# The state recurrence of a hybrid decoder layer's RWKV-7 mixer: chunk updates formed as affine maps for all chunks, then one scan over the three head pairs together

## The reference, cut to what matters

```
def step(S, inp):
    r_t, w_t, k_t, v_t, kk_t, a_t = inp
    sa = jnp.einsum('bhvk,bhk->bhv', S, -kk_t)
    S = (S * w_t[:, :, None, :]
         + sa[..., None] * (kk_t * a_t)[:, :, None, :]
         + v_t[..., None] * k_t[:, :, None, :])
    return S, jnp.einsum('bhvk,bhk->bhv', S, r_t)
```

## Time and profile before

| | |
|---|---|
| time, median of 3 runs | 876.85 us (874.28 to 879.99) |
| the profiled execution | 877.97 us, of which the span is 876.2 us |
| mean granted TensorE clock | 0.994 |
| PE busy | 840.4 us of the span |
| DVE, ACT, POOL busy | 281.8, 191.1, 101.3 us |
| meta recurrence and the three pairs | about 146.6 to 333.7 us of the span |

### The profile page before, as it was taken

The page is one execution under the profiler, slowest core; times in us unless marked ns, Lnnn a source line. Parts: engine busy times, 40 slices in busy tenths (PEclk is TensorE's granted clock), DMA queues, the critical chain, the costliest instruction groups (busy, mean ns, idle before and its releaser), DMA issues.

```text
span 876.2 us, 16200 instructions
## 1 busy us (share of the span) xinstructions
PE 840.4 (96%) x6939; PEld 473.6 (54%) x6939; DVE 281.8 (32%) x578; ACT 191.1 (22%) x380; POOL 101.3 (12%) x216
## 2 busy tenths in 40 slices
PE   9999999989999899899999999999999979999995
PEld 8888888766766454454544444444445533333331
DVE  5245710322323324712222434444411233121212
ACT  4224101131235122403121112080022201111110
POOL 8840000000005000111000000000000010222211
PEclk9999999999999999999999999999999999999998
DMA  7322146000000000481111111065390296999972
GB/s 218 89 60 85 49 96 195 2 3 3 3 2 2 3 27 25 99 204 48 49 48 49 49 48 49 25 240 166 122 358 26 76 399 245 326 389 394 388 254 99
DMA packets 76135, 109.76 MB, mean 125 GB/s; under 512 B 16891, under 2 KB 61067, under 8 KB 71968
## 3 DMA queue, kind: packets, MB, share of 16 engines
q1 hardware_dynamic: 71296, 93.22, 31.5%
q0 software_dynamic: 4768, 15.52, 6.1%
HBM read 100.32 MB, written 10.50 MB: 126 GB/s over the span
## 4 chain that ended last, share of the span: by engine, by line
PE 89%; DVE 4%; issue 2%; DMA 2%; ACT 1%; SPq 0%; POOL 0%; DVEq 0%; POOLq 0%; ACTq 0%
PE ps L1554 18%; PE ps L1922 10%; PE ps L1449 8%; PE ps L1531 8%; PE ps L1868 6%; PE ps L1621 6%; PE ps L1829 5%; PE ps L1948 5%; PE ps L1536 5%; PE ps L1748 1%; PE ps L1814 1%; PE ps L1909 1%; PE ps L1433 1%; PE ps L1788 1%; PE ps L1766 1%
## 5 line engine op out<-in xcount | busy, mean ns | idle before, releaser
L1554 PE MATMUL ps<-arena 128*128 128x512 f32 x304 | 141.3, 602 | 0.4 <-DMA arena<-in_w_in 0.4
L1554 PEld LDWEIGHTS ps<-arena 128*128 128x128 f32 x304 | 54.2, 189 | 62.1 <-issue 59.0
L1922 PE MATMUL ps<-arena 128*32 128x512 f32 x624 | 86.2, 599 | 0.5 <-DVE arena L1338 0.5
L1449 PE MATMUL ps<-arena 128*128 128x264 f32 x320 | 72.7, 386 | 0.0
L1449 PEld LDWEIGHTS ps<-arena 128*128 128x128 f32 x320 | 60.0, 189 | 11.6 <-ACT arena L757 0.7
L1531 PE MATMUL ps<-arena,h 128*128 128x264 f32 x256 | 63.4, 393 | 0.0
L1621 PE MATMUL ps<-arena 64*64 64x64 f32 x2208 | 50.9, 221 | 9.1 <-issue 5.2
L1621 PEld LDWEIGHTS ps<-arena 64*64 64x64 f32 x2208 | 44.6, 134 | 26.3 <-issue 18.5
L1868 PE MATMUL ps<-arena 128*128 128x512 f32 x128 | 56.2, 594 | 0.0
L1829 PE MATMUL ps<-yT_all,arena 128*128 128x512 f32 x112 | 50.2, 600 | 1.1 <-DMA arena<-in_w_p_fox 1.1
L1531 PEld LDWEIGHTS ps<-arena,h 128*128 128x128 f32 x256 | 46.6, 188 | 8.6
(11 more groups left out here) (349 smaller groups left out, 1023.5 us busy)
## 6 DMA issues: line engine op xcount, KB each, us to landing
arena<-in_moe_w_down SPq DMA_DIRECT2D x32, 512.0 KB, 6.0
arena<-in_moe_w_gate SPq DMA_DIRECT2D x13, 1024.0 KB
arena<-in_moe_w_up SPq DMA_DIRECT2D x13, 1024.0 KB
arena<-in_w_in SPq DMA_DIRECT2D x19, 512.0 KB, 3.8
arena<-in_w_in SPq DMA_DIRECT2D x5, 1024.0 KB, 6.5
h<-in_x SPq DMA_DIRECT2D x8, 512.0 KB, 5.8
arena<-in_w_out SPq DMA_DIRECT2D x1, 4096.0 KB, 13.2
h<-in_w_in SPq DMA_DIRECT2D x3, 1024.0 KB, 5.3
```

What stands on the lines that cost most here:

```text
L1449: ins = mm(ps[:, 2 * (n % 2) + hf, 0:HALF], w[:, c, j * P:(j + 1) * P], nT[:, c, hf * HALF:(hf + 1) * HALF], start=(c == 0), stop=(c == DC ...
L1554: ins = mm(ps[:, gate_bank(n), :], weights_of_gate(n)[:, c, :], nT[:, c, META:L], start=(c == 0), stop=(c == DC - 1))
L1922: ins = mm(ps[rs, bank, :].rearrange("p (h n) -> p h n", h=2), xgT[:, s, c, rs], w1[ws][:, :, c, :], start=(c == 0), stop=(c == DC - 1))
```

## The change

For each pair, instead of the scan, three further products are formed for all chunks at once, so that chunk c acts on its incoming state S as an affine map: new S = M S + K and y = R S + Y0.

- `w2`'s batch gets a second product (KtT x VT, the first half of K). After it come one batch of two products (M from W1 and BtT; first half of Y0), one of two products (R from W1 and RBT; second half of Y0) and one of a single product (second half of K): 16 + 32 + 32 + 16 matmuls more for each pair. DVE turns three of the results into place (`Rt`, `Bt`, `Kt`; 512 columns each), ACT copies Y0 out. Three steps of filler (`AFFINE_FILL`) stand behind them. The next pair's second turn batch waits for the DVE and ACT results.
- The scan then runs once, over the 8 chunks, with the three pairs inside: for each pair 2 matmuls for the state (not at the last chunk) and 2 for y, and one DVE operation for the new state. One step of `fill` follows each chunk. y is gathered in one PSUM bank for each pair and added to Y0 by DVE at the end (512 columns, three times).
- The six norms move from the scan of p = 1 into levels 3, 4, 5 of p = 1 and 1, 2, 3 of p = 2, in the place of 2 steps of `fill_qkv` each. With that and the scans' filler gone, `HEAD_FILL` grows from 111 to 139 steps. The gate filler behind the first two head sums shrinks from 5 and 8 steps to 3 and 7; those three steps are the filler behind the last pair's products.
- The two heads of a pair come out on swapped partition halves. So the bonus is copied with halves swapped (two copies for one), `ln_g` and `ln_b` load in four DMAs instead of two, and the RWKV projection weights in two DMAs for each block, so that a block takes 6 DMAs.

```
-        scan_fill = lambda p, c: (2, 0 if 1 <= c <= 6 else 4 if c == NCH - 1 else 2, 0)[p]
+        level_fill = lambda p, lv: (0 if (p, lv) in NORM_AT else 2) + LEVEL_FILL
...
+                for i in range(2):
+                    sp.dma_start(wpr[dc % 2][64 * i:64 * i + 64, 0:3, :], wp_r[:, cs].rearrange("(c h p) n -> h p c n", h=2, p=HD)[1 - i]).then_inc(s, 16)
...
                     groups_out(("H", p, lv))
+                    if (p, lv) == (1, 2):
+                        key_or_query_squares(0)
+                    if (p, lv) in NORM_AT:
+                        m = NORM_AT.index((p, lv))
+                        norm_root(m)
+                        if m < 5:
+                            key_or_query_squares(m + 1)
...
+                act.wait_ge(sem("q_psum"), p + 1)
+                done(a.activation(flat(Y0s[p]), ps[:, 6, :], ACT.Copy), "y0_ready")
+            act.wait_ge(sem("y_out_rwkv"), RC)
...
-            done(v.tensor_copy(tc_[:], tb[:]), "bonus_moved")
+            done(v.tensor_copy(tc_[0:64], tb[64:128]))
+            done(v.tensor_copy(tc_[64:128], tb[0:64]), "bonus_moved")
...
+                dve.wait_ge(sem("q_psum"), p + 1)
+                done(tt(body(Rt, p), body(Rt, p), bank(5), ALU.add), "affine_ready")
+                dve.wait_ge(sem("d_psum"), p + 1)
+                done(tt(body(Bt, p), bank(4), bc(ident2[:]), ALU.add), "affine_ready")
+                done(tt(body(Kt, p), bank(1), ends(p).broadcast_to([P, NCH, CH]), ALU.mult), "affine_ready")
+            for c in range(NCH - 1):
+                for p in range(RC):
+                    dve.wait_ge(sem("s_psum"), 1 + RC * c + p + 1)
+                    done(stt(Ss[p][:, c, :], ps[:, (0, 1, 4)[p], 0:CH], ends(p)[:, c, :], body(Kt, p)[:, c, :], ALU.mult, ALU.add), "S_ready")
...
+            for p in range(RC):
+                dve.wait_ge(sem("y_psum"), p + 1)
+                done(tt(yT[0][:, p, :], ps[:, 5 + p, :], Y0s[p].rearrange("p n t -> p (n t)"), ALU.add), "y_out_rwkv")
...
+                if p >= 1:
+                    pe.wait_ge(sem("affine_ready"), 3 * p)
+                    pe.wait_ge(sem("y0_ready"), p)
+                side_by_side((4, cm(Bt), cm(At), 0, 0), (6, cm(At), idq, 0, 1)).then_inc(sem("nt_psum"), 1)
...
-                side_by_side((0, um(TTm), um(Hm), 1, 0)).then_inc(sem("w2_psum"), 1)
+                side_by_side((0, um(TTm), um(Hm), 1, 0), (1, um(KtT), um(VT), 0, 0, "first")).then_inc(sem("w2_psum"), 1)
...
+                side_by_side((4, um(W1), um(BtT), 0, 0), (6, um(VT), um(RKT), 0, 1, "first"))
+                side_by_side((5, um(W1), um(RBT), 0, 0), (6, um(W2), um(RBT), 0, 1, "then")).then_inc(sem("q_psum"), 1)
+                side_by_side((1, um(BtT), um(W2), 0, 0, "then")).then_inc(sem("d_psum"), 1)
+                more(AFFINE_FILL)
+            pe.wait_ge(sem("affine_ready"), 3 * RC)
+            pe.wait_ge(sem("y0_ready"), RC)
+            for c in range(NCH):
+                for p in range(RC):
+                    if c >= 1:
+                        pe.wait_ge(sem("S_ready"), 1 + RC * (c - 1) + p + 1)
+                    state = S0[:, p, :] if c == 0 else Ss[p][:, c - 1, :]
+                    if c < NCH - 1:
+                        for q in range(2):
+                            ins = mm(ps[half(q), (0, 1, 4)[p], 0:CH], body(Bt, p)[half(q), c, :], state[half(q), :], start=True, stop=True)
+                        ins.then_inc(sem("s_psum"), 1)
+                    for q in range(2):
+                        ins = mm(ps[half(1 - q), 5 + p, c * CH:(c + 1) * CH], state[half(q), :], body(Rt, p)[half(q), c, :], start=True, stop=True)
+                    if c == NCH - 1:
+                        ins.then_inc(sem("y_psum"), 1)
+                fill(1)
             fill(4)
...
-                fill((5, DC)[c] if c < 2 else 0)
+                fill((3, DC - 1)[c] if c < 2 else 0)
```

More of the change, by code:

```diff
@@ L797, in _, with key_or_query_squares, norm_root @@
             groups_out(("meta", "S"))
+            def key_or_query_squares(m):
+                done(a.activation(tmp_shift[:, 0, :], QK[:, 4 + m, :], ACT.Square), "fsq_ready")
+            def norm_root(m):
+                act.wait_ge(sem("norm_psum"), m + 1)
+                if m >= 2:
+                    act.wait_ge(sem("fnorm_done"), m - 1)
+                q = slice(0, P) if m <= 3 else slice(64, P)
+                z = norm_rs[m % 2][q, :]
+                done(a.activation(z.rearrange("p (a b) -> p a b", a=2), ps[q, 0:2, 0:HALF], ACT.Ln, scale=1.0 / HD, bias=eps_c[q]), "fms_ready")
+                done(a.activation(z, z, ACT.Exp, scale=-0.5), "rs_ready")
             for p in range(RC):
                 act.wait_ge(sem("nt_psum"), p + 1)
-                done(a.activation(flat(AtT), ps[:, 1, :], ACT.Copy), "at_ready")
+                done(a.activation(flat(AtT), ps[:, 6, :], ACT.Copy), "at_ready")
                 groups_out(("turn", p))
@@ L811, in _ @@
                 act.wait_ge(sem("w1_psum"), p + 1)
-                done(a.activation(flat(W1Ts[p]), ps[:, 5, :], ACT.Copy), "w1_ready")
+                done(a.activation(flat(W1s[p]), ps[:, 5, :], ACT.Copy), "w1_ready")
                 done(a.activation(body(Bt, p), ps[:, 7, :].rearrange("p (n t) -> p n t", t=CH), ACT.Copy), "x_out")
@@ L1069, in _ @@
             bank = lambda b: ps[:, b, :].rearrange("p (n t) -> p n t", t=CH)
+            ends = lambda p: Pc[:, p, META + 1:].rearrange("p (n t) -> p n t", t=CH + 1)[:, :, CH:CH + 1]
             mbank = lambda b: ps[:, b, 0:RC * META].rearrange("p (n t) -> p n t", t=META)
@@ L1612, in _ @@
                 for q in range(2):
-                    o, r = ps[half(q), 7, p * CH:(p + 1) * CH], half(q, META)
+                    o, r = ps[half(q), 1, p * CH:(p + 1) * CH], half(q, META)
                     mm(o, mKT[r, p, :], mVT[r, p, :], start=True, stop=False, skip_group_check=True)
@@ L1616, in _, with product @@
             ins.then_inc(sem("s_psum"), 1)
-            def product(bank, q, c, lhs, rhs, f_in, f_out):
+            def product(bank, q, c, lhs, rhs, f_in, f_out, part=None):
                 r = half(q ^ f_in)
-                return mm(ps[half(q ^ f_out), bank, c * CH:(c + 1) * CH], lhs(r, c), rhs(r, c), start=True, stop=True)
+                start = c == 0 if part == "first" else part is None
+                return mm(ps[half(q ^ f_out), bank, c * CH:(c + 1) * CH], lhs(r, c), rhs(r, c), start=start, stop=part != "first", skip_group_check=part is not None)
             def side_by_side(*products):
@@ L1630, in _, with norm_sums @@
             idq = lambda r, c: ident2[r, :]
+            def norm_sums(m):
+                pe.wait_ge(sem("fsq_ready"), m + 1)
+                if m >= 1:
+                    pe.wait_ge(sem("fms_ready"), m)
+                for hf in range(2):
+                    ins = mm(ps[:, hf, 0:HALF], head_ones[:], tmp_shift[:, 0, hf * HALF:(hf + 1) * HALF], start=True, stop=True)
+                ins.then_inc(sem("norm_psum"), 1)
             for p in range(RC):
@@ L1696, in _ @@
-                    ins.then_inc(sem("y_psum"), 1)
-                    if p == RC - 1:
-                        fill(1)
-                    fill_qkv(scan_fill(p, c))
-                    if p == 1 and 1 <= c <= 6:
-                        pe.wait_ge(sem("fsq_ready"), c)
-                        if c >= 2:
-                            pe.wait_ge(sem("fms_ready"), c - 1)
-                        for hf in range(2):
-                            ins = mm(ps[:, hf, 0:HALF], head_ones[:], tmp_shift[:, 0, hf * HALF:(hf + 1) * HALF], start=True, stop=True)
-                        ins.then_inc(sem("norm_psum"), 1)
@@ L1820, in _ @@
             for dc in range(DC):
-                pe.wait_ge(sem(f"late{dc % 2}"), LATE_IN + 16 * 5 * (dc // 2 + 1))
+                pe.wait_ge(sem(f"late{dc % 2}"), LATE_IN + 16 * 6 * (dc // 2 + 1))
                 bank = lambda b: (0, 1, 2, 3, 4, 5)[(n + b) % 6]
```

97 lines of the change are left out of this document (25 added, 72 removed).

## The result

The changed kernel takes 850.01 us in the median of 4 runs (848.63 to 852.21), the kernel before beside it 876.6 us (874.28 to 879.99): a ratio of 0.9715 with an interval of 0.9688 to 0.9742. The profiled execution took 850.36 us, of which 848.4 are the span, against 877.97 before: 27.6 us less, where the sum had said 19.1. So 8.5 us are to be explained.

The account below looks back on a forecast made before the run. TensorE's work in written order plus its stalls was taken to set the end. Terms -34.9 + 5.7 + 9.9 - 1.4 + 1.2 + 0.4 = -19.1 us took the profiled 877.97 to 858.9, forecast as 858 us on the median's scale, range 852 to 868.

Parts of the forecast that it names:

- the removed term: Net cost of the three old scans, their filler taken off at its cost in a run: 34.9 us removed.
- rival D: Old scans' time is the matmuls themselves, not waits; new form's matmuls cost 47.8 us, time 891 us; chance 0.04.
- Rivals A and E: A: scan steps stay 2.27 us, 863.5, chance 0.15; E: pairs don't overlap, steps 3.1 us, 870, chance 0.04.
- Rival B: Scan steps of 1.43 us, p = 0 levels give 3.8 us, no new issue stalls: 853 us; chance 0.12.
- C: Norms don't hide in the levels; ACT's 2.05 us delays the next copy in six levels: +12.3, 870 us; chance 0.05.
- The new scan: One scan of 8 steps over three pairs, 1.6 us a step: 5.7 us added (4.4 to 11.4).
- The new products: Extra product batches after each pair's preparation, 3.3 us a pair: 9.9 us added (7.8 to 18.5).
- Levels and filler: Preparations with filler moved: p = 0 gains 2.0 us, p = 2 loses about 0.6; net -1.4 us (-3.8 to +0.6).
- Projection weights: A sixth DMA for each block's weight load: 0.4 us added (0 to 0.5).
- The end of the scan: Five gate steps, 4.5 us, cover y's additions and square, 4.2 us: hidden by 0.3 us; 0 to 0.5.
- Issue stalls: TensorE stalls without a releaser in the batches, 5.2 us, scaled by matmul record count: 1.2 us added (0 to 2.4).

Follow-up runs that it names:

- b_shift34: Kernel before with TensorE's instruction stream moved on by 34 matmuls (136 instructions) through altered warm-up; 869.66 us, ratio 0.9942.
- a_more_p2: Changed kernel with five instead of three filler steps behind each level's batch of p = 2, taken from the head; 847.07 us, ratio 0.9666.
- The four corners: Four kernels, norms moved in all: old recurrence or affine maps, each pair by pair or in lock step; 867.39, 850.96, 861.19, 850.01 us.
- a_oldstep: Changed kernel keeping the lock step but with the old recurrence instead of affine maps, the three new batches dropped; 850.96 us, ratio 0.9732.
- a_shift34: Changed kernel with TensorE's instruction stream moved by 34 matmuls ahead of all work; 854.84 us, ratio 0.9778 to the kernel before.
- b_bare: Kernel before without filler in the scans of the first and second pair, the 22 steps moved to the head; 876.46 us, ratio 0.9998.
- a_pairs: Changed kernel with affine maps kept but the scan run pair by pair instead of in lock step; 861.19 us, ratio 0.9864.

## Why the prediction was right, and where it was wrong

**The bound and the removed term hold.** TensorE's order sets the end, and the old scans were latency: busy time fell by 16.9 us with 204 records more, which refutes rival D (it wanted 47.8 us for the new matmuls; the products and the scan added 15.1). Rivals A and E are refuted by the step of 1.57 us. Rival B's 853 us is the nearest figure, but two of its three reasons did not come: the steps were not 1.43 us, and the levels gave not 3.8 us. The third, no new issue stalls, did, and went further than it had said. C is refuted as well: no wait for ACT in the norm levels. In level 5 of p = 1 ACT's norm work starts at 242.00, and its next copy, L830, follows at once and ends at 244.69. TensorE needs that copy for the batch of `w2`, which starts at 245.76: a cover of 1.1 us, as worked out. The timelines of ACT and of PE:

```profile
242.00 0.70 ACT L809 ACTIVATE arena<-ps,chan 128x528 f32<-128x528 f32 x1 [0.46 <-PE ps L1647]
...
243.41 0.64 ACT L801 ACTIVATE arena<-arena 128x528 f32<-128x528 f32 x1
244.09 0.60 ACT L830 ACTIVATE arena<-ps 128x512 f32<-128x512 f32 x1
```

```profile
245.76 1.11 PE L1631 MATMUL ps<-arena 64*64 64x64 f32 x64
```

**The new scan: right.** 11.52 - 7 x 0.859 = 5.5 us, forecast 5.7; steps of 1.57, forecast 1.6. TensorE waits for nothing in it. (The upper bound given there, 11.4, is 11.1 by its own formula.)

**The new products: right.** Less their filler the three windows leave 3.96, 3.51 and 3.14 us, 10.6 together, of which 1.0 is two issue stalls: 9.6, forecast 9.9 with the 0.2 for the grown `w2` batch that these windows leave out. The floor of about 25 ns between starts of matmuls, which the Trainium skill gives ("TensorE: Matmul & The Clock Gate", section "Wait — 56ns, not 53.3ns?"), is not seen here either: 160 records in 2.94 us are 18 ns each.

**Levels and filler: right for p = 0, too hopeful for p = 2.** Compared with `b_shift34`, which has no stalls, the preparation of p = 0 is 14.4 us (30.78 less 16.4 of filler) against 16.4 (29.76 less 13.4), the 2.0 us forecast. That of p = 1 is 0.3 longer (31.00 less 16.55 of filler and norm sums, against 31.49 less 17.34). p = 2 costs 1.3 more, where 0.6 was forecast, with four waits of 0.6 us on DVE; the kernel before has three of them there already (1.7 us), so one more came, as forecast, and some 0.6 us beside it. Net -0.4 where -1.4 was forecast. `a_more_p2` shows that the waits can be had back.

**Projection weights: too small.** The waits for that load went from 1.1 to 2.2 us, +1.1 where 0.4 was forecast and 0.5 was the bound:

```profile
PE ps L1837 <- DMA arena<-in_w_p_fox: 2.2, 2, 1.7
```

The size varies, but the six DMAs show: the eight profiled kernels that have them wait 1.4 to 2.8 us, the six with five DMAs 0.7 to 1.1. **The end of the scan** was hidden by 0.7 us: ACT ends the square of y at 312.23, the filler runs until 312.95.

```profile
310.74 1.49 ACT L841 ACTIVATE arena<-yT_all 128x1536 f32<-128x1536 f32 x1 [16.54 <-DVE yT_all L1126]
```

**The step that failed is "Issue stalls":** 5.2 x 576 / 2592 = 1.2 us added. It took a stall at a fixed place of the stream for one that comes by the number of matmuls. The working even had the right cause at hand (a sequencer crossing between blocks) and concluded only that the term might then be zero. Never asked was what becomes of the 5.2 us that were there already, and of what they cost beyond their idle time. Measured, on the profiled executions: the stalls cost the kernel before 8.8 us in that stretch. The change has 1.3 us of idle time from them left, which at the same ratio of cost to idle time (8.8 to 5.2) is some 2.2 us, an estimate. So the term is between -7.5 and -6.6 in place of +1.2, a miss of 7.8 to 8.7 where 8.5 was to be explained. That this comes out so close is partly luck of the one execution of before that was profiled, which had more stalls than others. On the medians 8.0 us are to be explained (850.0 against 858). The shift is worth 5.4 us there, the term thus -4.1 to -3.2, and the miss 4.4 to 5.3; about 3 us stay open.

The same check from the other side: the sum without this term is -20.3; between the two profiles that are nearly free of stalls, `b_shift34` with 869.66 us and the change with 850.36 (its 1.3 us of stalls taken off: 849.1), lie 20.6 us. The single terms as measured above (-34.9, which no run measures again, +5.5, +9.6, -0.4, +1.1) make -19.1 without the stalls, so 1.5 us stay unassigned among them. Later waits move by as much on their own: that for the rows of `n_rows`, in the mixture of experts, is 2.3 us in the profile before, 0.9 in that of `b_shift34` and 1.1 after. On the medians, of the 26.6 us that the change gains 4 to 5 are the stalls that it happened to move, and about 20 are its own in the place where its stream stands; with both streams shifted it was 14.8.

**The change's reasons, taken apart,** look otherwise than the prediction had them. It priced the affine maps as what shortens the step (three operations of DVE to one) and the lock step as given. The four corners show the reverse: lock step is nearly all of it. Three chains in turn already keep TensorE busy for 22.12 of the 22.13 us of the scan of `a_oldstep`, without a wait, so a shorter chain has nothing left to shorten; it saves only matmuls in the scan, and these cost as much in the new batches.

## What to carry to other kernels

A stretch of latency-bound steps is cured first by interleaving independent chains, which was worth 11 to 16 us here; see whether that alone fills the engine before paying for algebra that shortens the chain. If stalls without a releaser stand at equal distances in the count of an engine's instructions, they belong to how the stream is cut into blocks and to whether the blocks come in time, not to the work: number them before an edit is costed, and when two kernels are compared, run one of them shifted by half a block, or part of their difference may be nothing but position: here the shift took 5.4 us from one kernel and gave the other 4.8. And a price by count is only right for what comes by count.

## What was not expected of the hardware

- Stalls at block ends in dense batches: gaps of 0.3 to 1.2 us, 10 of them at 23 crossings in the kernel before, none at 21 after a shift of 136 instructions. Elsewhere they are rare (0.3 us of idle time once at L1545, 0.5 us once at L1566 of `a_shift34`). Dense batches use instructions up fastest, 64 PE records and as many weight loads within 1.09 us, but that is not enough for a stall: the crossings of `b_shift34` fall in batches just as dense. What goes with every stall that was looked at is a load that ended 1.2 to 1.6 us before it did. What makes the load late is open.
- Small matmuls with waits between them let the granted clock fall. In `b_bare` it went from 1.00 to 0.50, from 2.4 to 1.2 GHz, within the bare scan, in which PE was busy for 3.48 of the first 5.52 us, and a step grew from 1.88 to 2.27 us. In `a_pairs` it fell in the same way and the step grew from 0.79 to 0.94 us:

```profile
296.06:299.90 3.84, 1.73 (x41) 1.04 (x40) 1.36 (x5) 0.00 (x0) 0.00 (x0) 0.96 0.44 124
300.10:311.00 10.90, 7.08 (x90) 3.88 (x90) 2.85 (x10) 0.00 (x0) 0.00 (x0) 0.50 0.01 2
```

In the kernel before, the scan that `b_bare` strips has its two steps of filler in each chunk and stays at 1.00; so does the change, whose scan has a gate matmul in every step and no wait. So filler between dependent steps does two things: it fills the wait, and it keeps the clock.
- Three products side by side over the array's quarters run no faster than two and then one: 2.94 us for 160 records both times.
